# A fused two-block kernel: first loads, zero products, and the way from the MLP to the first expert gather

## The reference

```python
def peer(h, w_query, sub_keys, u, v):        # per token, 8 heads
    q = einsum('btd,dq->btq', hx, w_query)   # 2 x 128 numbers for each head
    s = einsum('bthpc,hpnc->bthpn', q, sub_keys)
    top_s, top_i = lax.top_k(s, PEER_TOPK)   # 16 of 128, for each half
    cand_s = top_s[..., 0, :, None] + top_s[..., 1, None, :]   # 256 sums
    best_s, best_pos = lax.top_k(cand_s, PEER_TOPK)            # 16 experts
    gate = softmax(best_s)
    act = gelu(einsum('btd,bthkd->bthk', hx, u[expert]))
    return einsum('bthk,bthkd->btd', gate * act, v[expert])
```

## Time and profile before

| | us |
|---|---|
| median of 3 runs (lowest, highest) | 1858.69 (1857.79, 1860.07) |
| the profiled execution | 1860.88 |
| its span | 1858.8 |
| first projection starts | 15.88 |
| second part starts | 137.99 |
| last product of the MLP ends | about 375.6 |
| first gather is issued | 418.42 |
| last gather has landed | 1851.97 |

### The profile page before, as it was taken

One profiled execution on the slowest core, in us unless ns is written; L12 is line 12 of the kernel. 1 busy time (PEld: TensorE's weight loads), 2 busy tenths in 40 slices (PEclk: granted clock), 3 DMA queues, 4 the chain that ended last, 5 costly groups with the idle time before them and its releaser, 6 DMA issues.

```text
span 1858.8 us, 21506 instructions
## 1 busy us (share of the span) xinstructions
PE 1381.9 (74%) x7036; PEld 562.7 (30%) x7036; DVE 1168.2 (63%) x2684; ACT 597.7 (32%) x1523; POOL 550.5 (30%) x629
## 2 busy tenths in 40 slices
PE   7979999987785555589778875686787855556656
PEld 6836566654341010123122222121232210101010
DVE  4831244057785767776787537865985478777765
ACT  2421111124442333343343333333543333332332
POOL 2002052004342333332332323322333233333332
PEclk9989999999996766789887887798788977766676
DMA  9049397619999999999999999999999999999997
GB/s 331 26 149 363 115 400 268 246 47 361 420 420 419 422 421 421 422 407 416 420 392 403 420 417 421 394 413 417 421 391 414 419 421 412 420 422 421 421 416 314
DMA packets 118239, 681.28 MB, mean 367 GB/s; under 512 B 11838, under 2 KB 14016, under 8 KB 50160
## 3 DMA queue, kind: packets, MB, share of 16 engines
q0 software_dynamic: 78336, 553.68, 72.4%
q1 hardware_dynamic: 39792, 126.23, 17.8%
HBM read 678.30 MB, written 1.05 MB: 365 GB/s over the span
## 4 chain that ended last, share of the span: by engine, by line
DMA 38%; PE 31%; DVE 10%; ACT 5%; issue 4%; DVEq 2%; POOL 2%; ACTq 1%; another core or an unknown queue 0%; POOLq 0%
DMA big<-in_peer_uv,expert 33%; PE ps L583 7%; PE ps L1785 6%; PE ps L1796 6%; PE ps L741 5%; DVE big L596 5%; DMA normed<-in_peer_uv,expert 3%; PE ps L568 2%; DMA big<-in_w_kv 2%; POOL big L554 2%; DVEq L462 2%; PE ps L327 1%; ACT L604 1%; ACT L627 1%; ACT placed L627 1%
## 5 line engine op out<-in xcount | busy, mean ns | idle before, releaser
L583 PE MATMUL ps<-big,placed 128*32 128x512 f32 x1992 | 601.0, 799 | 373.4 <-ACT placed L631 356.9
L596 DVE CUSTOM_DVE_ANT_0 big<-big,ps 128x1024 f32<-128x1024 f32 x498 | 595.7, 1220 | 336.6 <-DMA big<-in_peer_uv,expert 312.6
L554 POOL DMA_INDIRECT big<-in_peer_uv,expert x498 | 474.7, 953 | 1029.3 <-PE ps L583 848.1
L627 ACT ACTIVATE placed<-sel,dots 128x32 f32<-128x32 f32 x512 | 163.8, 320 | 781.7 <-DVE dots L596 762.0
L583 PEld LDWEIGHTS ps<-big,placed 128*32 128x32 f32 x1992 | 83.0, 123 | 805.2 <-ACT placed L631 706.4
L741 PE MATMUL ps<-big 128*128 128x512 f32 x384 | 186.7, 622 | 10.7 <-DMA big<-in_w_kv 8.7
L631 ACT ACTIVATE placed<-placed,gate 128x32 f32<-128x32 f32 x512 | 165.1, 322 | 36.0 <-issue 1.0
L1785 PE MATMUL ps<-ua,big 128*128 128x256 f32 x512 | 117.3, 383 | 0.0
L1796 PE MATMUL ps<-big,sc 128*128 128x512 f32 x256 | 115.5, 595 | 0.0
L741 PEld LDWEIGHTS ps<-big 128*128 128x128 f32 x384 | 69.1, 194 | 125.0 <-issue 102.6
L1785 PEld LDWEIGHTS ps<-ua,big 128*128 128x128 f32 x512 | 98.4, 192 | 27.1 <-issue 15.0
(11 more groups left out here) (342 smaller groups left out, 1302.6 us busy)
## 6 DMA issues: line engine op xcount, KB each, us to landing
big<-in_mlp_w SPq DMA_DIRECT2D x16, 2048.0 KB, 13.6
big<-in_peer_wq SPq DMA_DIRECT2D x2, 8192.0 KB, 26.8
big<-in_w_kv SPq DMA_DIRECT2D x32, 512.0 KB
big<-in_peer_wq SPq DMA_DIRECT2D x32, 512.0 KB
big<-in_w_in SPq DMA_DIRECT2D x5, 2048.0 KB, 17.8
big<-in_peer_uv,expert POOLq DMA_INDIRECT x530, 13.2
big<-in_w_q SPq DMA_DIRECT2D x16, 512.0 KB
big<-in_w_o SPq DMA_DIRECT2D x16, 512.0 KB
```

Source lines behind the costliest of these rows:

```text
L554: nc.gpsimd.indirect_dma_start(out=pair_row(n), out_offset=None, in_=rows, in_offset=bass.IndirectOffsetOnAxis(ap=expert[:, n // TOPK % DE ...
L583: last = nc.tensor.matmul(acc[r:r + TOK, :], placed[:, n % RING, :], pair_row(n)[:, D + BANK * half:D + BANK * (half + 1)], start=(opens a ...
L596: nc.vector.tensor_tensor_reduce(out=row, in0=row, in1=rows_x, scale=1.0, scalar=0.0, op0=ALU.mult, op1=ALU.add, accum_out=dots[:, u % 2, ...
L627: a.activation(to, sel32[:], ACT.Gelu, scale=dots[:, u % 2, k:k + 1])
```

## The change

In the first part the 19 small loads become two, from one array that the host has put together, and `x` tile 1 is loaded behind them. PE runs 7 products with a zero matrix, transposes the vectors, runs 3 more, transposes both tiles, runs 7 more. DVE copies the vectors between the norms of tile 0 and tile 1. 28 zero products stand ahead of `x1_transposes(1)` and 7 behind. POOL writes `zeros` earlier.

In the MLP the seeds are gone: the first and the last `down` open and close the sums. The row of pooling scales is loaded during the MLP, DVE multiplies it into the pooling weights there, and `add_mixed` is one instruction. Both `pooled_out` of tile 0 stand ahead of the norm of tile 1. 7 zero products stand ahead of `ffn0_transposes(0)` and 3 behind; the two halves of those transposes are signalled, copied and used one by one. `first_experts` searches 8 of each half and 8 of 64 sums, and releases the first 8 gathers; the rest of unit 0's search runs behind it. `FIRST` goes from 4 to 2, `unit_rows(0)` and the second tile's norm move ahead, and all four stages of unit 1 go into the turns 0 and 1.

```diff
-            last.then_inc(S("ffn0_t"), 1)
+                if k % 4 == 3:
+                    last.then_inc(S("ffn0_t"), 1)
 
         def ffn0_transposes_out(dve, t):
 
             at = first_column(t)
-            dve.wait_ge(S("ffn0_t"), t + 1)
             for j in range(2):
+                dve.wait_ge(S("ffn0_t"), 2 * t + j + 1)
                 nc.vector.tensor_copy(hnt[:, 4 * j:4 * j + 4, at:at + P], cut(bank(4 * t + j), 0, 4, P))\
                     .then_inc(S("ffn0_t_out"), 1)
...
+                if u == 0 and k % 4 == 0:
+                    pe.wait_ge(S("ffn0_t_out"), k // 4 + 1)
...
-        FIRST = 4
+        FIRST = 2
 
         def peer_head_pe(pe, other_tile):
 
-            pe.wait_ge(S("ffn0_t_out"), 2)
             pe.wait_ge(S("peer_wq0_loaded"), 32)
             queries_pe(pe, 0)
             query_columns_pe(pe, 0)
...
             scores0_pe(pe, 0)
             other_tile()
             queries_pe(pe, 1)
+            pe.wait_ge(S("h1"), 2)
+            unit_rows(pe, 0)
             query_columns_pe(pe, 1)
             scores0_pe(pe, 1)
-            queries_pe(pe, 2)
-            queries_pe(pe, 3)
-            for u in range(2, FIRST):
-                query_columns_pe(pe, u)
-                scores0_pe(pe, u)
-            pe.wait_ge(S("h1"), 2)
-            unit_rows(pe, 0)
             ffn0_transposes(pe, 1)
...
+        HALF = TOPK // 2
+
+        def first_experts(dve):
+
+            v = nc.vector
+            scores_ready(dve, 0)
+            for half in range(2):
+                part = slice(P * half, P * (half + 1))
+                v.max(half_v[:, half, 0:HALF], scores[:, 0, part])
+                dve.drain()
+                v.max_index(half_i[:, half, 0:HALF], half_v[:, half, 0:HALF], scores[:, 0, part])
+                dve.drain()
+            v.tensor_scalar(half_f[:, 0, 0:HALF], half_i[:, 0, 0:HALF], KEYS, None, ALU.mult)
+            v.tensor_copy(half_f[:, 1, 0:HALF], half_i[:, 1, 0:HALF])
+            square = [P, HALF, HALF]
+            sums = work[:, 2, 0:HALF * HALF]
+            v.tensor_tensor(sums.rearrange("p (i j) -> p i j", i=HALF), half_v[:, 0, 0:HALF].unsqueeze(2).broadcast_to(square),
+                            half_v[:, 1, 0:HALF].unsqueeze(1).broadcast_to(square), ALU.add)
+            dve.drain()
+            v.max(best[:, 0, 0:HALF], sums)
+            dve.drain()
+            v.max_index(best_at[:, 0:HALF], best[:, 0, 0:HALF], sums)
+            dve.drain()
+            winners_to_experts(dve, 0, 0, HALF, HALF)
+            v.tensor_tensor(expert[:, 0, 0:HALF], picked[:, 0, 0:HALF], picked[:, 1, 0:HALF], ALU.add)\
+                .then_inc(S("first_experts_ready"), 1)
...
+        def winners_to_experts(dve, u, lo, hi, side):
+
+            n, bits = hi - lo, int(math.log2(side))
+            v.tensor_scalar(ints[:, 0, lo:hi], best_at[:, lo:hi].bitcast(I32), bits, None, ALU.logical_shift_right)
+            v.tensor_scalar(ints[:, 1, lo:hi], best_at[:, lo:hi].bitcast(I32), side - 1, None, ALU.bitwise_and)
+            dve.drain()
+            v.tensor_copy(pos_f[:, :, lo:hi], ints[:, :, lo:hi])
+            dve.drain()
+            for w in range(2):
+                is_at = work[:, w, 0:n * side].rearrange("p (i j) -> p i j", i=n)
+                v.tensor_tensor(is_at, pos_f[:, w, lo:hi].unsqueeze(2).broadcast_to([P, n, side]),
+                                iota16[:, 0:side].unsqueeze(1).broadcast_to([P, n, side]), ALU.is_equal)
+            dve.drain()
+            for w in range(2):
...
+                v.tensor_tensor(is_at, is_at, half_f[:, w, 0:side].unsqueeze(1).broadcast_to([P, n, side]), ALU.mult)
+            dve.drain()
+            for w in range(2):
...
+                v.tensor_reduce(picked[:, w, lo:hi], is_at, X, ALU.add)
...
             def top16(values, index, source, rest):
-                done(v.max(values[:, 0:8], source))
-                done(v.max_index(index[:, 0:8], values[:, 0:8], source))
+                if u > 0 or stage == 2:
+                    done(v.max(values[:, 0:8], source))
+                    done(v.max_index(index[:, 0:8], values[:, 0:8], source))
                 done(v.match_replace(rest, values[:, 0:8], source, MASKED))
                 done(v.max(values[:, 8:16], rest))
                 done(v.max_index(index[:, 8:16], values[:, 8:16], rest))
...
+                if u == 0:
+                    winners_to_experts(dve, u, HALF, TOPK, TOPK)
+                    v.tensor_tensor(expert[:, 0, HALF:], picked[:, 0, HALF:], picked[:, 1, HALF:], ALU.add)\
+                        .then_inc(S("experts_ready"), 1)
+                    return
...
-                if n % TOPK == 0:
+                if n == 0:
+                    pool.wait_ge(S("first_experts_ready"), 2)
+                elif n == HALF or n % TOPK == 0:
                     pool.wait_ge(S("experts_ready"), n // TOPK + 1)
...
-            for stage in range(4):
-                route(dve, 0, stage)
+            first_experts(dve)
             other_tile()
-            for stage in range(2):
-                route(dve, 1, stage)
+            route(dve, 0, 0)
+            route(dve, 0, 1)
+            ffn0_norm(dve, 1)
+            route(dve, 0, 2)
+            ffn0_transposes_out(dve, 1)
+            route(dve, 0, 3)
             gates_of(dve, 0)
-            ffn0_norm(dve, 1)
-            ffn0_transposes_out(dve, 1)
...
-                for t in range(NT):
-                    sp.dma_start(h[:, t, :], x_v[:, t, :]).then_inc(S(f"x{t}_loaded"), 16)
-                rows = [(conf_dw_w[0], CONF_K), (sconv_w[0], SC_K), (lru_conv_w[0], LRU_K), (conf_dw_b, 1),
...
-                gains = [pre_mix_g, pre_mlp_g, norm_mix[0:1], kv_norm.rearrange("(o n) -> o n", o=1), norm_mix[1:2]]
+                sp.dma_start(h[:, 0, :], x_v[:, 0, :]).then_inc(S("x0_loaded"), 16)
+                sp.dma_start(vrows[0:V_CHAN, :], vectors[0:V_CHAN, :]).then_inc(S("vectors_loaded"), 16)
+                sp.dma_start(grows[0:VECS - V_CHAN, :], vectors[V_CHAN:VECS, :]).then_inc(S("vectors_loaded"), 16)
+                sp.dma_start(h[:, 1, :], x_v[:, 1, :]).then_inc(S("x1_loaded"), 16)
...
-                for t in range(NT):
+                def x_norm(t):
                     dve_inverse_rms(dve, t, P, t, "x")
                     step(dve, v.tensor_scalar(hn[:, t, :], h[:, t, :], stats[:, 9 + t:10 + t], None, ALU.mult), "x_normed")
+
...
+                x_norm(0)
                 dve.wait_ge(S("vectors_t"), 1)
                 chain(v.tensor_copy(vec[:, 0:V_CHAN], bank(7)[:, 0:V_CHAN]))
                 step(dve, v.tensor_copy(vec[:, V_CHAN:VECS], bank(7)[:, P:P + VECS - V_CHAN]), "vectors_ready")
+                x_norm(1)
...
+                def zero_products(b, n):
+                    for _ in range(n):
+                        m.matmul(cut(bank(b), 0, 4, P), zeros[:], zeros[:].unsqueeze(1).broadcast_to([P, 4, P]),
+                                 start=True, stop=True)
...
+                pe.wait_ge(S("constants_ready"), 3)
+                zero_products(6, 7)
+                pe.wait_ge(S("vectors_loaded"), 16 * 2)
                 m.transpose(bank(7)[:, 0:V_CHAN], vrows[0:V_CHAN, :], ident[0:V_CHAN, 0:V_CHAN])
                 n = VECS - V_CHAN
                 m.transpose(bank(7)[:, P:P + n], grows[0:n, :], ident[0:n, 0:n]).then_inc(S("vectors_t"), 1)
+                zero_products(6, 3)
+                x_transposes(0)
+                x_transposes(1)
+                zero_products(6, 7)
...
+                zero_products(1, 28)
                 x1_transposes(1)
+                zero_products(2, 7)
...
+                sp.dma_start(scale_row, pool_scale[0].partition_broadcast(P)).then_inc(S("pool_w_loaded"), 16)
                 sp.dma_start(poolw, pool_v).then_inc(S("pool_w_loaded"), 16)
-                sp.wait_ge(S("down_done"), DFF // P + FT)
-                sp.dma_start(scale_row, pool_scale[0].partition_broadcast(P)).then_inc(S("scale_loaded"), 16)
+                sp.wait_ge(S("down_done"), DFF // P)
...
-                    step(dve, v.tensor_tensor(tmp[:, t, :], tile_banks(t), scale_row, ALU.mult), "dve_order")
-                    step(dve, v.tensor_tensor(h[:, t, :], h[:, t, :], tmp[:, t, :], ALU.add), "h1")
+                    step(dve, v.tensor_tensor(h[:, t, :], h[:, t, :], tile_banks(t), ALU.add), "h1")
...
+                dve.wait_ge(S("pool_w_loaded"), 32)
+                own = poolw.rearrange("p (g k) n -> p g k n", k=2)
+                for k in range(2):
+                    v.tensor_tensor(own[:, :, k, :], own[:, :, k, :], scale_row.rearrange("p (g n) -> p g n", n=GW), ALU.mult)\
+                        .then_inc(S("pool_w_scaled"), 1)
...
+                pooled_out(0, 1)
+                dve.wait_ge(S("pool_w_scaled"), 2)
                 pool_norm(2, P, 1, hn[:, 1, :])
-                pooled_out(0, 1)
-                dve.wait_ge(S("scale_loaded"), 16)
...
-                for b in range(4):
-                    last = seed(b, True)
```

(8 more changed lines are left out.)

87 lines of the change are left out of this document (38 added, 49 removed).

## The result

| | median us | from, to | runs |
|---|---|---|---|
| before | 1859.38 | 1857.79, 1860.16 | 4 |
| after | 1843.88 | 1841.12, 1847.51 | 4 |

The ratio is 0.9919 (0.99 to 0.9938). The change saves 15.5 us; 23.35 were forecast, and the time lies just above the range. The profiled execution after took 1843.97 us; its span of 1841.9 us is 16.9 shorter than that of the earlier trace rows, and is read here step by step.

A forecast was written before the change was run, and what follows sets the result against it. The DMA-bound gather stage moves fixed bytes, so time depends on when the first gather is issued and whether the DMA engines run dry. Seven terms sum to 23.35 us off 1858.69, giving 1835.3 us; range 1830 to 1843.

The forecast's parts named there:

- 1, the start: Kernel start: earlier weight loads, projections from 12.05 us and at full clock; 6.0 us saved (2.5 to 6.3).
- 2, the transposes: Border of the two parts: transposes behind the 28 zero products run at full clock; 0.9 us saved.
- 3, the seeds: Start of the second part: the four seeds ahead of up(0) go; 1.7 us saved.
- 4, clock in the MLP: First MLP products: less idling ahead, half of the half-clock loss counted as gain; 0.85 us saved (0 to 1.7).
- 5, MLP's end to scores: From the MLP's end to the scores: closing seeds gone, transposes and queries faster; 4.2 us saved (1.8 to 4.6).
- 6, the search: DVE's search between scores and first gather shrinks from 10.9 to 4.6 us; 6.3 us saved (5 to 7).
- 7, the pauses: Behind the first gather: the DMA engines' pauses vanish, ninth gather 16 us behind the first; 3.4 us saved (1 to 4.2).
- the norm of tile 1 ends at 8.9: At the start: DVE ends the vector copies and tile 1's norm at 8.9 us, gain products end at 12.0.
- the chunk lands by 11.5 ... Then the input decides: At the start: first weights, issued at about 2.4 us, land by 11.5, so the input sets the projections' start.
- The rival of a clock that doesn't stay up: PE's clock falls at short gaps, so less is gained up to the scores: 17.0 us saved, 1841.7, chance 0.18.
- the new wait for the vectors: At the start: DVE waits for the vectors ahead of tile 1's norm; vectors past 7 us could cost up to 1.3.
- The rival of a ring that runs dry early: Behind the first gather: DVE, ACT and PE meet in the first turns, DMA stops again; 1840.7 us, chance 0.13.

The follow-up runs named there:

- e4_seeds_back: Changed kernel with four zero products put back at the start of the second part, ahead of the MLP; 1843.90 us, one run.
- e1_bank_free: Changed kernel with ACT handing over the MLP's banks at the second part's start, not after its norm of the meta tokens; 1842.54 us, ratio 0.9897.
- e5_tail_warm: Changed kernel with four zero products of PE behind each of the last eleven slot values but the very last; 1842.57 us, ratio 0.9923.
- c1_same_again: The changed kernel run again without any edit, on the chip of group 2; 1844.25 us, ratio 0.9899.
- e6_old_search: Changed kernel with the search of before for the first unit, all 16 experts in four stages; 1847.57 us, ratio 0.9918.
- e8_two_then_hold: Changed kernel with POOL's third gather also waiting until PE has done unit_rows(0); 1843.38 us, ratio 0.99.
- e2_x1_first: Changed kernel with the load of x's tile 1 issued second, ahead of the two loads of vectors; 1845.5 us, ratio 0.9919.
- e7_gathers_held: Changed kernel with POOL's first gather also waiting until PE has done unit_rows(0); 1847.8 us, ratio 0.9922.
- e10_best_seeds: Changed kernel with the zero products of e4_seeds_back, the third-gather wait of e8_two_then_hold and the zero products of e5_tail_warm; 1840.72 us, ratio 0.9914.

## Why the forecast was off

The terms in us, read from the first profile against that of before, and over all executions of the changed start, MLP and search:

| term | forecast | first profile | others |
|---|---|---|---|
| 1, the start | 6.0 | 3.5 | 3.3 to 5.1 |
| 2, the transposes | 0.9 | 0.9 | 0.9 |
| 3, the seeds | 1.7 | 0.0 | 0.0 |
| 4, clock in the MLP | 0.85 | 0.3 | -1.2 to 0.3 |
| 5, MLP's end to scores | 4.2 | 5.1 | 5.1 |
| 6, the search | 6.3 | 6.1 | 6.1 |
| 7, the pauses | 3.4 | 1.8 | -1.5 to 2.1 |
| the end | 0 | -0.8 | -0.9 to 0 |
| sum | 23.35 | 16.9 | |

(Term 7 is the way from the first gather to the last dot product against 1433.55 us; the others' terms leave out the kernels whose edit touches them.)

**Term 3 failed, and was an error of reading.** I took the step from the seeds to up(0) in the earlier trace rows for their duration. It was ACT's norm of the meta tokens, which PE waits for either way. `e4_seeds_back` (no cost) and `e1_bank_free` (1.5 us) show it. The prediction did not ask what PE would wait for next once they were gone.

**Term 1 failed in three links.** The first is "the norm of tile 1 ends at 8.9". I had tile 1 landed when ACT was free at 6.1. It is the fourth load and is used at 6.7 to 7.8 in all ten executions in which it stands there. The second is "the chunk lands by 11.5 ... Then the input decides". The first 2 MB of weights are issued 5.2 us earlier than before and land only 2.7 us earlier, at 13.07 (15.75 before), and at 12.4 to 13.4 in every profiled execution of a changed kernel. So 12.05 was out of reach even with tile 1 in time. In `e5_tail_warm`, where tile 1 came earliest of the ten, nothing but the weights is waited for:

```profile
13.46 3.71 PE L1490 MATMUL ps<-sc,big 128*128 128x256 f32 x16 [1.54 <-DMA big<-in_w_in]
```

The third is the clock ahead of the projections. Where tile 1's transposes and the seven zero products behind them ran at full clock and the weights were there, the projections began 3.0 us behind the norm of tile 1 (`c1_same_again`, `e4_seeds_back`, `e6_old_search`, `e8_two_then_hold`), and where both ran at half or nearly so, 4.1 to 4.9 us (`e1_bank_free`, `e2_x1_first`, `e7_gathers_held`, `e10_best_seeds`). So the first projection starts at 13.0 to 14.9. Behind it the clock is worth 1.6 to 2.2 of the 2.2 us forecast. The rival of a clock that doesn't stay up was right on this place. Its total of 17.0 us is near the 16.9 of the two profiles by luck: it put terms 2 and 5 at 0 and 1.8, and they measured 0.9 and 5.1. That the new wait for the vectors could be a danger was wrong in this order of loads: they are there by 5.0 to 5.6 us. With the rule of the Trainium skill, page "DMA: Bandwidth & Descriptors", section "Why a DMA increments its semaphore by 16 and not by 1", by which the prediction had them on 15 and 14 engines and early, the trace agrees, but no row tells the engines apart.

**Term 7 failed as a size, and in its rival.** The forecast had the ninth gather 16 us behind the first; it was 17 to 18 where PE ran through, 22.5 to 24.5 where it did not. The rival of a ring that runs dry early had the right sign and place where PE was late, but not the cause, which I didn't see: neither DVE nor the order, but PE's instructions. The kernel before has the same in ACT, which in the earlier trace rows stands behind the seventh gather's 8.69 us. So the pause that the change was credited with removing is in part one that comes and goes between executions of either kernel (1429.8 and 1433.5 us before; 1431.5 to 1435.1 after). Against 1429.8 us, the kernel before with the shorter pause, this term has the other sign: the stage takes 1.6 us longer on the same chip (`e5_tail_warm`). In the undelayed first profile after, the pauses of the first 30 us lost 2.9 us of bytes against 6.5 before (windows of 5 us against 422 GB/s), which is the term; but the last dot product waits for the last of the data, and that gained less. This is the view of the DMA's bytes over 62 us in 40 slices, before (from 1818 on) and after (from 1800 on):

```profile
GB/s 418 418 428 418 423 423 423 423 418 423 428 412 423 423 423 423 423 375 137 53 32 16 0 0 5 85 0 5 0 0 0 0 0 0 0 0 0 0 0 0
```

```profile
GB/s 423 423 423 418 418 423 423 423 423 423 412 423 423 423 423 418 423 201 42 26 26 16 0 0 0 0 85 0 5 0 0 0 0 0 0 0 0 0 0 0
```

After, the full rate ends at 1827, and for 7 us a rest trickles at the rate of about one of 16 engines (422 / 16 = 26). The last 0.25 MB take 6.7 us, and took 5.1 before. That most of it is one engine's share is inferred from the rate. The Trainium skill, page "DMA: Bandwidth & Descriptors", section "Latency and other measured facts", says that two of the DMA engines are usually slower than the others under gathers issued by GpSimd, and gives a cause as a guess. The trace agrees in so far as about one engine's share comes last, by 7 us here, and does not tell which engine it is.

**Terms 2, 5 and 6 held.** Term 5 came out 0.9 better. Counted from the first ACTIVATE behind the MLP, PE's sums of tile 1 start 12.4 us later, against 13.4 before, since `pooled_out(0, 1)` no longer stands behind the norm of tile 1; the prediction had the 0.86 us of the seeds in this gain and 0.1 beyond it.

Of the 6.4 us that the profile falls short of the forecast, terms 1 and 3 make 4.2, term 7 and the end 2.4, and term 4 0.6, less 0.8 won in terms 5 and 6. The forecast took the good case of terms 1, 3 and 7 at once, and its range was narrower than these were uncertain.

**Open:** why PE's instructions come late under gathers in all five profiled executions of the changed order with nothing held back on two chips, and in neither on two others, although the first profile of before has ACT late. What differs between the chips was not taken apart. The trace shows that they wait for no engine; it does not show what is being loaded. The Trainium skill, page "Advanced Engine Details and Errata", section "ISA Cache", gives the cache of an engine's instructions lines of 16 KB, 256 instructions each. The profile's queue of kind instruction has such packets (0.92 MB in 56), which agrees, but in both the delayed and the undelayed execution one of them stands between 406 and 408 us.
